# Moving the SBUF tiles: the operands of most matmuls start 64 bytes past a multiple of 128

## The reference

```python
for l in range(DEPTH):                       # DEPTH = 2
    pl = modulate(xl, g_mix[l], sh1, sc1) @ w_in[l]          # 512 tokens
    pc = modulate(xc, g_mix[l], csh1, csc1) @ w_in[l]        # 256 tokens
    oa_l, ob_l, oc_l = ...                   # three groups of heads
    xl = xl + gt1 * (concat(oa_l, ob_l, oc_l) @ w_out[l])
    xl = xl + gt2 * swiglu(modulate(xl, g_ffn[l], sh2, sc2), w_ffn_in[l], w_ffn_out[l])
    if l < DEPTH - 1:                        # the context tokens go on only in layer 0
        xc = ...                             # the same two updates
return xl
```

## Time and profile before

| | |
|---|---|
| time, median of 3 runs | 2223.57 us (2223.35 to 2224.59) |
| the profiled execution's own time | 2229.28 us |
| its span, first to last instruction | 2227.5 us |
| mean granted TensorE clock | 0.978 |
| TensorE matmuls busy | 2092.5 us, 94% |
| weight loads / VectorE / ScalarE / GpSimd busy | 77% / 54% / 34% / 29% |
| DMA | 74 GB/s over the span |

### The profile page before, as it was taken

One profiled execution on the slowest core, in us unless ns is written; L12 is line 12 of the kernel. 1 busy time (PEld: TensorE's weight loads), 2 busy tenths in 40 slices (PEclk: granted clock), 3 DMA queues, 4 the chain that ended last, 5 costly groups with the idle time before them and its releaser, 6 DMA issues.

```text
span 2227.5 us, 30035 instructions
## 1 busy us (share of the span) xinstructions
PE 2092.5 (94%) x11738; PEld 1721.1 (77%) x11738; DVE 1200.1 (54%) x2143; ACT 751.1 (34%) x1221; POOL 644.7 (29%) x820
## 2 busy tenths in 40 slices
PE   7888999989989999999999998889998979999998
PEld 4777788866667888888888877778866657888886
DVE  7467513567885776177537566653368854212111
ACT  4333323456663211111111234423265643212221
POOL 1210311220002343334333430131220014555555
PEclk9999989999999999999999999998899999999999
DMA  7300432110002233233223310021110002322322
GB/s 289 105 15 29 142 110 69 38 48 10 10 10 67 76 130 116 76 114 136 91 95 116 102 50 10 20 69 39 38 48 20 10 19 76 95 95 95 98 96 100
DMA packets 76242, 165.58 MB, mean 74 GB/s; under 512 B 5192, under 2 KB 46664, under 8 KB 75088
## 3 DMA queue, kind: packets, MB, share of 16 engines
q1 hardware_dynamic: 75728, 163.28, 22.0%
q10 hardware_dynamic: 384, 0.47, 0.1%
HBM read 161.63 MB, written 2.10 MB: 74 GB/s over the span
## 4 chain that ended last, share of the span: by engine, by line
PE 79%; DVE 11%; issue 4%; ACT 4%; PEld 1%; POOL 1%; DMA 0%; PEldq 0%; DVEq 0%; SPq 0%; ACTq 0%; POOLq 0%
PE psum L1097 22%; PE psum L1099 21%; PE psum L1098 21%; PE psum L1696 1%; DVE naptlo L2105 1%; PE psum L1148 1%; PE psum L1726 1%; PE psum L1336 1%; PE psum L1465 1%; PE psum L1451 1%; PE psum L1402 1%; DVE maplo L2356 1%; PE psum L1221 1%; PE psum L1189 1%; POOL wlo L539 1%
## 5 line engine op out<-in xcount | busy, mean ns | idle before, releaser
L539 POOL TENSOR_TENSOR wlo<-raw,whi 128x256 fp32r<-128x256 f32 x816 | 644.5, 820 | 1572.5 <-ACT whi L564 1572.5
L1097 PE MATMUL psum<-hhi,whi 128*128 128x512 f32 (+1 forms) x1640 | 589.0, 359 | 16.8 <-DVEq L1899 8.6
L1098 PE MATMUL psum<-hlo,whi 128*128 128x512 f32 (+1 forms) x1640 | 579.3, 353 | 0.0
L1099 PE MATMUL psum<-hhi,wlo 128*128 128x512 f32 (+1 forms) x1640 | 578.8, 353 | 0.0
L564 ACT ACTIVATE whi<-raw 128x1024 fp32r<-128x1024 f32 x204 | 215.7, 1059 | 877.3 <-PE psum L1099 870.9
L1097 PEld LDWEIGHTS psum<-hhi,whi 128*128 128x128 f32 x1640 | 312.9, 191 | 73.2 <-issue 18.8
L1099 PEld LDWEIGHTS psum<-hhi,wlo 128*128 128x128 f32 x1640 | 312.5, 191 | 42.7
L1098 PEld LDWEIGHTS psum<-hlo,whi 128*128 128x128 f32 x1640 | 313.0, 191 | 40.5 <-issue 0.2
L2538 DVE TENSOR_TENSOR ffuf<-ffsa,psum 128x768 f32<-128x768 f32 (+1 forms) x44 | 36.1, 821 | 313.0 <-ACT ffsa L1047 306.2
L2523 DVE SCALAR_TENSOR_TENSOR ffmacc<-wm,csil,ffmacc 128x256 f32<-128x256 f32 x336 | 188.3, 601 | 10.4 <-DVE ffmacc L2523 5.3
L1097 PE MATMUL psum<-uhi,whi 128*128 128x512 f32 (+1 forms) x528 | 189.1, 358 | 3.5 <-DVE ulo L2542 1.9
(11 more groups left out here) (331 smaller groups left out, 3401.0 us busy)
## 6 DMA issues: line engine op xcount, KB each, us to landing
raw<-w_stream SPq DMA_DIRECT2D x204, 512.0 KB, 3.7
wm<-w_mod SPq DMA_DIRECT2D x80, 512.0 KB, 4.2
wm<-w_mod SPq DMA_DIRECT2D x8, 1024.0 KB, 13.1
xres<-x_t SPq DMA_DIRECT2D x8, 384.0 KB, 7.1
out<-xres SPq DMA_DIRECT2D x8, 256.0 KB, 3.2
consts<-c_f SPq DMA_DIRECT2D x1, 353.0 KB, 3.4
narpb<-rpb ACTq DMA_DIRECT2D x2, 120.0 KB
mlmask<-c_gate ACTq DMA_DIRECT2D x2, 108.0 KB
```

The source lines that it names most:

```text
L539: nc.gpsimd.tensor_tensor(wlo[:, q % 2, c:c + UW // 4], raw[:, q % RAW, c:c + UW // 4], whi[:, q % 2, c:c + UW // 4], ALU.subtract).then_i ...
L1097: mm(dst, ah, bh, start=first, stop=False)
L1098: mm(dst, ah, bl, start=False, stop=False)
L1099: return mm(dst, al, bh, start=False, stop=last)
```

## The change

It moves tiles in the SBUF. No instruction, shape, wait or DMA is added, taken away or put in another order. Tiles are placed one behind another, in the order in which the program asks for them, from byte 16,512 of each partition on (129 × 128). Before, this was the residual, `hhi`, `hlo`, the weights, the constants and small tiles, and then the shared region. After, it is a filler of 64 bytes, `hhi`, `hlo`, the shared region, the residual, the weights, the constants. The start of each, in bytes, with its place within 128 and within 256 bytes:

| tile | before | in 128, in 256 | after | in 128, in 256 |
|---|---|---|---|---|
| `hhi` | 41,088 | 0, 128 | 16,576 | 64, 192 |
| `hlo` | 65,664 | 0, 128 | 41,152 | 64, 192 |
| `uhi`, `ulo` | 135,744, 160,320 | 64, 64 | 69,824, 94,400 | 64, 192 |
| `maqhi`, `maqlo`, `makhi`, `maklo`, `cqhi`, `cqlo`, `ckhi`, `cklo`, `naohi`, `naolo` | 131,648 to 190,016 | 64, 64 | 65,920 lower | 64, 192 |
| `mlo` | 215,936 | 0, 128 | 150,016 | 0, 0 |
| `maphi`, `maplo` | 208,512, 214,656 | 0, 128 | 142,592, 148,736 | 0, 0 |
| `whi` | 106,624 | 0, 128 | 204,352 | 64, 64 |
| `wlo` | 114,816 | 0, 128 | 212,544 | 64, 64 |
| `xres` | 16,512 | 0, 128 | 163,392 | 64, 64 |
| `raw` | 90,240 | 0, 128 | 187,968 | 64, 64 |
| `consts` | 123,008 | 0, 128 | 220,736 | 64, 64 |

The whole shared region moves down by 65,920 bytes, which is 515 × 128, so the tiles in it keep their places within 128 bytes. All steps inside these tiles from one matmul's operand to the next are multiples of 256 bytes. The small input `cin`, read once at the start, now uses part of `amix` that is written only later. Of the 9,256 fp32r matmuls, 64 have both operands at 32 past a multiple of 128, before and after. Of the other 9,192, before, 5,976 had both at a multiple of 128, 2,136 the moving one alone at 64 past it, 176 the stationary one alone, 904 both. After, 8,608 have both at 64 past a multiple and 584 the stationary one alone.

```diff
@@ -50,6 +50,7 @@
 HEAD_SLOT = {0: 0, 2: 1, 1: 2, 3: 0}
 RING = 3
 RING_AT = 20832
+SCOPES = RING_AT + RING * UW + 512
@@ -84,29 +85,9 @@
-        xres = sb("xres", [P, KT, TOK])
+        sb("half_line", [P, 16])
         hhi = sb("hhi", [P, KT, TOK], fp32r)
         hlo = sb("hlo", [P, KT, TOK], fp32r)
-        raw = sb("raw", [P, RAW, UW])
-        whi = sb("whi", [P, 2, UW], fp32r)
-        wlo = sb("wlo", [P, 2, UW], fp32r)
-        consts = sb("consts", [P, 3 * P + 256 + 64 + 2])
...
-        cin = sb("cin", [P, KT, 2])
...
@@ -197,6 +178,28 @@
         RNG, NRM, NA, ML, MA, FF = (scope(f) for f in (ring_scope, norm_scope, na_scope, ml_scope, ma_scope, ff_scope))
+        sb("scopes", [P, SCOPES])
+        xres = sb("xres", [P, KT, TOK])
+        raw = sb("raw", [P, RAW, UW])
+        whi = sb("whi", [P, 2, UW], fp32r)
+        wlo = sb("wlo", [P, 2, UW], fp32r)
+        consts = sb("consts", [P, 3 * P + 256 + 64 + 2])
...
+        cin = amix[:, 1, 0]
```

More of the change, by code:

```diff
@@ L199, in build @@
         RNG, NRM, NA, ML, MA, FF = (scope(f) for f in (ring_scope, norm_scope, na_scope, ml_scope, ma_scope, ff_scope))
+        sb("scopes", [P, SCOPES])
[4 more added lines that the diff above has]
+        consts = sb("consts", [P, 3 * P + 256 + 64 + 2])
+        ident = consts[:, 0:P]
+        ones = consts[:, P:2 * P]
+        ones2 = consts[:, 2 * P:3 * P]
+        band = consts[:, 3 * P:3 * P + 256]
+        colmask = consts[:, 3 * P + 256:3 * P + 320]
+        msel = consts[:, 3 * P + 320:3 * P + 322]
+        identb = sb("identb", [P, P], bf16)
+        dirmask = sb("dirmask", [P, 2, P], bf16)
+        lc = sb("lc", [P, DEPTH, NCOL])
+        mods = sb("mods", [P, DEPTH, 48, 2])
+        amix = sb("amix", [P, DEPTH, 2, KT, 2])
+        cin = amix[:, 1, 0]
+        csil = sb("csil", [P, KT, 32])
+        eps = sb("eps", [P, 1])
+        stat = sb("stat", [P, 2, 8])
+        tab = sb("marope", [P, SEQ])
         def norm_bufs(l, which):
```

## The result

The changed kernel takes 2238.84 us (median of 4 runs, 2234.85 to 2243.97), the kernel before in the same batch 2223.46 (4 runs): a ratio of 1.0076, 95% interval [1.0055, 1.0098]. It is slower by 15.4 us, where 3.7 us less was forecast. Timed again later, the ratio was 1.0060 [1.0039, 1.0081].

A forecast was written before the change was run, and what follows sets the result against it. TensorE's matmul turns were taken to bound the kernel (busy 94% of the span). Terms of -3.5, -0.2, -0.4 and +0.4 made -3.7 us, from 2223.57 to 2219.9 us; own range 2216 to 2223, 8 in 10: 2213 to 2239.

The forecast's parts named there:

- step 1: `hhi`, `hlo` against the weights, either one moving: operands alike within 128 bytes before and after, so 0 us.
- Turns by place: Trace of before, 512 and 256 columns: operands alike within 128 bytes take 227 and 120 ns, unlike 233 and 113.
- The difference counts within 256 bytes: Rival, chance 0.22: `hhi` and `whi` end 128 apart; +4.9 us, or +15 to +20; middle +10, 2234 us.
- Step 2: `uhi`, `ulo` in layer 1: 528 turns of 512 columns go from 233.3 to 226.7 ns, 3.5 us less.
- Step 3: `uhi`, `ulo` in layer 0: 512-column turns lose 6.6 ns, 256-column turns gain 6.7; taken as -0.2 us.
- Step 4: Projections from `cq` and `nao`: 120 turns of 512 columns in layer 1 at half the gain, -0.4 us.
- Step 5: `maphi`, `maplo` past `hhi` and `mlo` past weights become unlike: 2.0 ns more per turn, partly hidden, +0.4 us.
- Steps 6 and 7: ScalarE, VectorE, GpSimd pay nothing for the new places; the weights' DMA landing 64 past stays under TensorE: 0 each.
- Everything unaligned is slower: Rival, chance 0.09: every 512-column turn goes to 233.3 ns, 256-column ones stay; +20.7 us, 2244 us.
- The new distance is a better one: Rival, chance 0.12: 233 ns or less at 512 columns, 113.3 at 256, -15.8 us; half of it, 2216 us.
- Nothing changes: Rival, chance 0.13: 16-byte lines, or the 6.6 ns belong to something else in the output stage; 2223.6 us.

The follow-up runs named there:

- the matmuls alone: Separate kernel that only copies its input, then runs 48 fp32r matmuls per line at chosen operand places: 226.7 ns per 512-column turn at distance 0, 233.3 at 64.
- Distances 0, 192 and 240: Changed kernel re-laid so stationary minus moving address, modulo 256, is 0, 192 or 240 for `hhi` and weights: 2223.46, 2220.24 and 2221.18 us.
- the three at distance 128: Changed kernel timed again, 2237.89 us; changed kernel without its 64-byte filler, 2237.25 us; order of before with weights moved to 128 apart, 2236.09 us.

## Why the prediction was wrong

The step that failed is step 1 of "The change part by part", with the reading under "Turns by place" that it rests on: "If the difference within 128 is what counts: 0 us". The distance counts within 256 bytes. The step put at nothing what cost nearly the whole loss: `h` and `w` went from distance 0 to 128, both 64 past a multiple of 128, and in layer 1 the turn of 512 columns went from 227.1 to 233.2 ns. The figures of before were read rightly; they held distances 0, 64 and 192 and no 128, so the period could be either. One fact in them spoke for 256, and was used only in a rival: 64 gave 233.3 and 192 gave 228.7, while under a period of 128 the two would be one distance and should have had one figure. By itself it was a weak sign, as 15 turns are few and distance 192 has since shown 233.3 as well.

The measured 2238.8 us lies just inside the range for 8 in 10, 2213 to 2239. That is no merit of the sum: its own range ended at 2223, and the upper end came from the rivals.

- Step 1, 0 us forecast: +15.3 at 512 columns, -1.8 at 256. In the rival "The difference counts within 256 bytes" the 512-column term had the right sign and was a third too large: 3,120 x 6.6 = +20.7, where the counted turns have 5.2 ns and +15.3. Its 256-column term had -6.7 ns, the price of distance 64; distance 128 has -0.8. Its other case, where those turns gain little, was +15 to +20, and the chip gave +15.
- Step 2, -3.5 us: 0. `u` past `w` went from distance 64 to 128, not to the pace of the aligned pair, and the two cost the same, 233.3. Where the pair did come to distance 0 (the changed kernel with `RING_AT` lower), its long stretches had 226.7: the gain of this step, at a distance that the change did not give.
- Step 3, -0.2 us: +1.9. The 256-column turns left 114.7 for 118.9 (+2.2), and the 512-column ones stayed (-0.3).
- Step 4, -0.4 us: -0.1, for the same reason as step 2.
- Step 5, +0.4 us: +0.4 (`mlo` past `w` 228.3 to 233.2 in layer 1, `maphi` past `hhi` +0.7 ns, on 309 counted turns). The size held by luck, as both prices were others: `mlo`, now at distance 64, paid 4.9 ns there and not 2.0, and `maphi` less than 2.0.
- Steps 6 and 7, 0: right. Busy times as before, ScalarE's 812 ns still 812, DMA 0.30 of a window in layer 1 against 0.29.

Of the other rivals: "Everything unaligned is slower" would have given the same 233.3 at the place it named, and 2244 us, not far off. The kernels that take alignment and distance apart refute it: all aligned at distance 128 has a ratio of 1.0067, all unaligned at distance 0 has 1.0000. "The new distance is a better one" fell with 233.3, though its kind seems to exist, as distance 192 hints. Its working has a slip: the -15.8 us need 226.7 ns at 512 columns, since 233 there would add 20.7 and cancel it. "Nothing changes" fell with the matmuls alone, which pace by distance with no output stage around them.

What the prediction took from the page, that by it the sum would be zero, does not hold for the matmuls alone. The Trainium skill, SBUF — State Buffer, section Specifications (TRN2), gives lines of 16 bytes, and section Who interferes with whom gives TensorE independent read ports for the moving operand and for weight loads. If these were all that counts, a distance of 64 bytes would cost nothing. Measured: 226.7 ns at distance 0 against 233.3 at 64, with no other engine at work. No run shows whether the ports or the lines are behind it.

What stays open: why a distance makes a turn longer; what decides between the two levels of one distance (113.3 and 117.8 at 256 columns; 228.9 and 233.3, 226.7 and 228.3 at 512); and why the kernels with shorter turns gave back less than their sum. Distances 0, 192 and 240 promised 4.7, 7.6 and 6.7 us and their medians showed 0, 3.2 and 1.1, with intervals of about 3 to 4 us to either side. A part of that is the clock, which differs from execution to execution (0.973 to 0.985). A straight line of time against granted clock, fitted afterwards through all 123 executions of the later batches, with a level of its own for each kernel and, for the kernel before, on each chip, falls by 1.4 us for each 0.001. Compared at equal clock by this line, the three are 2.4, 4.1 and 3.1 us below before, each give or take 1.4, and the three at distance 128 are 14.3, 13.3 and 13.2 above, give or take 1.8. So the gains are real by this estimate, and still only about half of the sums of turns; no run tells where the rest goes.

## What to carry to other kernels

A sum over turns of matmuls, read start to start, found the loss to within a microsecond or two (15.3 against 15.4, 13.9 against 12.7), but promised gains about twice as large as they came. TensorE's busy time as a whole shows the loss too; the busy time and the mean length of the groups hide which turns it is in. When a layout is moved, tabulate for each large pair the stationary address less the moving one, modulo 256, and compare that, not the alignment: here, at 512 columns, 0 is the best, 192 mostly costs 2 ns of 227, and 64 and 128 cost 5 to 7; at 256 columns 64 and 192 are the best or, at their slower level, 2 ns below 0. Before a rule is read out of a trace ("the difference within 128"), list which values the trace holds of it; a case that it lacks is worth a rival with the larger period's price.

## What the hardware showed that was not expected

- The pace of back-to-back fp32r matmuls, each with a new stationary tile of 128 columns, depends on the distance of the two operands modulo 256 bytes: 226.7 to 234.2 ns at 512 columns, 113.3 to 120.0 at 256. Readings 4 bytes apart differ by up to 6.6 ns. The two widths don't follow each other: distance 0 is the best at 512 and the worst at 256. Distance 192 has read 228.9 in eight stretches of the matmuls alone with full-width weights and 233.3 in one.
- A stretch settles into a cycle. Single turns at distance 0 read 226 and 227; at 64 they read 233 and 234 in a stretch of the kernel before and alternate between 231 and 236 in another, with the same mean of 233.3; the changed kernel's input alternates 229 and 238, and at distance 128 without the filler seven turns repeat (241, 232, 231, 232, 228, 230 and 232).
- Narrower weights even the distances out (a spread of 1.2 ns with 32 columns loaded) at 231 ns, above the best level with 128 columns, 226.7.
